# Moving the stationary operands of the token-major products 32 bytes below the weights' place within 512 bytes

## The chip, the cores and the metric

The program runs on one core of one Trainium2 chip. The metric is the device time of one execution in microseconds, as the median of several runs. One more execution was recorded by the hardware profiler, and all rows below come from that one.

## The reference

Two transformer blocks are chained on 256 tokens of width 1024. All of it is float32.

```python
# block 1, two layers
for layer in range(2):
    xn = rms_norm(h, attn_norm_g[layer])
    u_ssm, u_g, v_g, q, k, v = split(xn @ w_in[layer])          # 256,256,256,512,512,512 columns
    mixed = concat([s5_mixer(u_ssm), spatial_gating(u_g, v_g), diff_attention(q, k, v)])
    h = h + mixed @ w_out[layer]
    xn = rms_norm(h, ffn_norm_g[layer])
    a = causal_conv3(xn @ w_up[layer])                          # 2 x 2816 columns
    gate, val = split(a)
    h = h + (gelu(gate) * val) @ w_down[layer]
# block 2, one layer
n = rms_norm(x, g_pre)
a_qkv, bq, bk, bv, mq, ga, gb, gm, mg = split(n @ w_in_2)       # 12 chunks of 512 for a, mg and so on
branches = [windowed(a_qkv) * silu(ga), grouped(bq, bk, bv) * silu(gb), memory(mq, mem) * silu(gm)]
merged = sum(sigmoid(mg_i + b_i) * (branch_i @ w_br_i))
out = x + rms_norm(merged @ w_out, g_post)
```

## The kernel before

**The stream of weights.** All the large products share one stream of 294 pairs of weight tiles. A pair is 128 partitions by 1024 float32 columns (512 KB). The SP queue loads it into `raw` (one of 7 slots). ScalarE rounds it to a high part `whi` (6 slots, L1177), VectorE makes the rest, `wlo = raw - whi` (7 slots, in the memory of `raw`, L1873). The activations are split in the same way into a high and a low part: the normed input into `xthb` and `xtlb`, the gated units into `hth` and `htl`, the branch outputs into `oth` and `otl`, the normed memory into `memh` and `meml`. TensorE then makes three products in `fp32r` for each tile: high by high, high by low, low by high.

**Two forms of product.** `project` and `pair_products` issue them in one of two forms.

- Feature-major (`fm=True`, L646 to L648): the *weights* are the stationary operand (128 columns, 512 bytes of a partition) and the *activations* are the moving one, 256 columns (1024 bytes). This form serves `ssm_u`, the 22 `up` units but one, `km`, `mq`, `gb`, `gm` and `ga`.
- Token-major (L655 to L657 in `pair_products`, and L603, L593, L586 in `tile_pairs`, which makes one tile of tokens at a time): the *activations* are stationary (128 columns, 512 bytes) and the *weights* move, 512 columns (2048 bytes). This form serves q, k, gmlp, v, out, down, `up0_0`, vm, bq, the nine chunks of a, mg, the branch products and wo. `bkv` has this form with 256 moving columns.

Each matmul has a load of its stationary operand of its own (LDWEIGHTS, shown as engine PEld), and the load for the next matmul runs while the present one streams.

**Two places for the normed input.** `xthb` and `xtlb` each hold the normed input at one of two offsets: `xth`, `xtl` at offset 0 and `fth`, `ftl` at offset 8 elements, which is 32 bytes. The first is what attention, mixer, output and second-block products read; the second is written by the norm ahead of the up products and read by them alone.

```python
(xth, xtl), (fth, ftl) = ([b[:, o:o + KD * TOK].rearrange("p (k n) -> p k n", k=KD) for b in (xthb, xtlb)]
                          for o in (0, 8))
```

**Places within 512 bytes.** SBUF tensors are laid out one behind the other, so a start is the sum of the sizes ahead of it. Three unused tensors (`lines`, `lines1`, `lines2`) fill up to a multiple of 512 bytes. With the sizes in the code, the starts modulo 512 are these (the low parts lie as the high ones):

| tensor | bytes within 512, before | after |
|---|---|---|
| `whi`, `wlo` (all slots), `xres`, `xn` | 0 | 0 |
| `xth`, `xtl` | 0 | 480 |
| `fth`, `ftl` | 32 | 32 |
| `memh`, `meml` | 0 | 0 |
| `hth`, `htl`, `acc`, `gtd` | 0 | 480 |
| `aqT`, `va`, `oth`, `otl`, `merged`, `gpost` | 0 | 480 |
| `kmT`, `vm`, `colv` | 64 | 480 |
| `rowv`, `cst` (identity, rotation tables) | 384 | 288 |

**Order of work.** The order on every engine is written out by hand; small products and transposes of attention and of the mixer are set between the pairs of the stream. Nothing of that order depends on where a tensor lies.

Of the kernel before, what the change touches and what calls it, by code (L numbers as in the profile page):

```python
# [20 lines left out]
P = 128  # L21
TOK, TT = 256, 2
D, KD = 1024, 8
# [14 lines left out]
F32, F32R = mybir.dt.float32, mybir.dt.float32r  # L38
# [101 lines left out]
def build(nc, weights, x, mem, cols, rows, lams, bmerge, consts, amask, bexp, cexp, wst, wglu, out):  # L140
    with ExitStack() as ctx:
        def sbt(stack, name, shape, dt=F32):
            return stack.enter_context(nc.sbuf_tensor(name, shape, dt))
# [3 lines left out]
        def sem(name):  # L147
            if name not in sems:
# [10 lines left out]
        xres = sbt(ctx, "xres", [P, TT, D])  # L159
        xn = sbt(ctx, "xn", [P, TT, D])  # L160
        xthb = sbt(ctx, "xthb", [P, KD * TOK + 128], F32R)
        xtlb = sbt(ctx, "xtlb", [P, KD * TOK + 16], F32R)
        (xth, xtl), (fth, ftl) = ([b[:, o:o + KD * TOK].rearrange("p (k n) -> p k n", k=KD) for b in (xthb, xtlb)]
                                  for o in (0, 8))
        kmT = sbt(ctx, "kmT", [P, MH, TOK])
        vm = sbt(ctx, "vm", [P, TT, 512])

# [17 lines left out]
        hb = sbt(ctx, "hb", [P, 4])  # L185
        nlam = sbt(ctx, "nlam", [P, LAYERS])
        lamv = sbt(ctx, "lamv", [P, 8])
        sbt(ctx, "lines", [P, 120])

        def col(name, i=0, n=None):  # L190
            a, b = COL[name]
# [66 lines left out]
        mix.close()  # L258
        ffs = ExitStack()
        one.enter_context(ffs)  # L260
        sbt(ffs, "lines1", [P, 96])
        hth = sbt(ffs, "hth", [P, FT, TOK], F32R)
        htl = sbt(ffs, "htl", [P, FT, TOK], F32R)
        acc = sbt(ffs, "acc", [P, 2, 4, TOK])
# [5 lines left out]
        two = ExitStack()  # L270
# [15 lines left out]
        mqT = sbt(bm, "mqT", [P, MH, TOK])  # L286
        bm.close()
        gt = sbt(two, "gt", [P, TT, 3 * D])
        sbt(two, "lines2", [P, 96])
        att = ExitStack()  # L290
        two.enter_context(att)
        aqT = sbt(att, "aqT", [P, 2, NG, 4, TOK])
# [2348 lines left out]
```

## Time and profile before

| | us |
|---|---|
| median of 3 runs | 965.48 (964.66 to 966.56) |
| span of the profiled execution | 964.3 |
| mean granted TensorE clock | 0.999 of full |

The profiled execution is known by its span; the median of the runs lies 1.2 us above it. In the rows, PE is TensorE's matmul queue and PEld its loads of the stationary operand. The time shown for one matmul includes its way through the pipeline, so several overlap: what one costs in a stream is the distance between two starts, and this is how the rows are used here.

### The profile page before, as it was taken

Reading aid. Unit: us, or ns where it says so; the run is one execution under the profiler, and the core shown is the slowest. Engines: PE = TensorE matmul, PEld = TensorE weight load, DVE = VectorE, ACT = ScalarE, POOL = GpSimd, SP = SyncE. Lnnn points to the kernel's source line nnn. Section 1 sums busy time; section 2 is a strip of 40 time slices with the busy share of each in tenths; the row PEclk is TensorE's granted clock in tenths of the full one; section 3 lists DMA queues with packets and bytes.
Section 4 is the critical chain, followed back from the end, with each engine's and each line's share of the span. In section 5 each row is a group of like instructions: output and inputs, shape, how many; then the busy total and the mean of one; then the engine's idle time right before and its main releaser. Section 6 shows DMA issues by size and latency. Waiting matters only on the chain.

```text
span 964.3 us, 15784 instructions
## 1 busy us (share of the span) xinstructions
PE 953.3 (99%) x6119; PEld 837.1 (87%) x6123; DVE 687.4 (71%) x1081; ACT 567.6 (59%) x960; POOL 232.1 (24%) x189
## 2 busy tenths in 40 slices
PE   8999999999999999999999999999999999999997
PEld 6887899999888888899999988999778889888886
DVE  7987878786765877857777754748576755666885
ACT  7967666676855657756666544535454445555733
POOL 5560203536500110302445500021131300000030
PEclk9999999999999999999999999999999999999999
DMA  8642466656664634466566565665545445754462
GB/s 299 227 131 68 142 219 186 189 178 184 194 197 152 180 127 153 133 188 192 180 194 178 195 196 154 216 202 173 166 139 153 153 144 170 199 162 155 154 180 82
DMA packets 48618, 165.96 MB, mean 172 GB/s; under 512 B 6560, under 2 KB 7072, under 8 KB 48544
## 3 DMA queue, kind: packets, MB, share of 16 engines
q1 hardware_dynamic: 48544, 164.95, 54.9%
q8 instruction: 49, 0.80, 0.3%
q14 instruction: 25, 0.20, 0.1%
HBM read 162.83 MB, written 1.05 MB: 170 GB/s over the span
## 4 chain that ended last, share of the span: by engine, by line
PE 88%; ACT 4%; POOL 3%; DVE 3%; issue 1%; DMA 1%; SPq 0%; DVEq 0%; POOLq 0%; ACTq 0%
PE PJ L655 14%; PE PJ L657 13%; PE PJ L656 13%; PE PJ L648 10%; PE PJ L647 10%; PE PJ L646 10%; PE PJ L593 2%; PE PJ L603 2%; PE PJ L586 2%; PE T L1118 1%; ACT sm L1378 1%; PE T L1109 1%; ACT whi L1177 1%; DMA raw<-weights_in 1%; DVE wlo L1873 1%
## 5 line engine op out<-in xcount | busy, mean ns | idle before, releaser
L1873 DVE TENSOR_TENSOR wlo<-raw,whi 128x1024 fp32r<-128x1024 f32 x294 | 368.7, 1284 | 87.2 <-ACT whi L1177 84.8
L1177 ACT ACTIVATE whi<-raw 128x1024 fp32r<-128x1024 f32 x294 | 301.6, 1059 | 64.9 <-DMA raw<-weights_in 62.5
L646 PE MATMUL PJ<-xthb,whi 128*128 128x256 f32 x832 | 233.7, 281 | 0.0
L648 PE MATMUL PJ<-xthb,wlo 128*128 128x256 f32 x832 | 233.4, 281 | 0.0
L647 PE MATMUL PJ<-xtlb,whi 128*128 128x256 f32 x832 | 232.4, 279 | 0.0
L655 PE MATMUL PJ<-whi,xthb 128*128 128x512 f32 (+1 forms) x424 | 170.8, 403 | 0.3 <-DVE wlo L1873 0.2
L657 PE MATMUL PJ<-whi,xtlb 128*128 128x512 f32 (+1 forms) x424 | 164.0, 387 | 0.0
L656 PE MATMUL PJ<-wlo,xthb 128*128 128x512 f32 (+1 forms) x424 | 164.0, 387 | 0.0
L647 PEld LDWEIGHTS PJ<-xtlb,whi 128*128 128x128 f32 x832 | 157.0, 189 | 0.3
L646 PEld LDWEIGHTS PJ<-xthb,whi 128*128 128x128 f32 x832 | 157.0, 189 | 0.3
L648 PEld LDWEIGHTS PJ<-xthb,wlo 128*128 128x128 f32 x832 | 156.9, 189 | 0.0
L1798 POOL TENSOR_TENSOR gtd<-acc 128x512 f32<-128x512 f32 x22 | 93.6, 4255 | 166.4 <-ACT acc L1502 158.7
L2256 DVE SCALAR_TENSOR_TENSOR acc<-PJ,colv,acc 128x255 f32<-128x255 f32 (+1 forms) x168 | 69.2, 475 | 48.6 <-ACT acc L1497 47.9
L655 PEld LDWEIGHTS PJ<-whi,xthb 128*128 128x128 f32 x424 | 79.7, 188 | 20.5 <-issue 4.3
L657 PEld LDWEIGHTS PJ<-whi,xtlb 128*128 128x128 f32 x424 | 79.7, 188 | 16.8
L656 PEld LDWEIGHTS PJ<-wlo,xthb 128*128 128x128 f32 x424 | 79.9, 188 | 14.0
L1497 ACT ACTIVATE acc<-PJ,colv 128x256 f32<-128x256 f32 x84 | 40.6, 564 | 77.6 <-PE PJ L648 77.6
L655 PE MATMUL PJ<-whi,hth 128*128 128x512 f32 x144 | 56.0, 389 | 0.0
L657 PE MATMUL PJ<-whi,htl 128*128 128x512 f32 x144 | 56.0, 389 | 0.0
L656 PE MATMUL PJ<-wlo,hth 128*128 128x512 f32 x144 | 56.0, 389 | 0.0
L1852 POOL TENSOR_TENSOR merged<-merged,gt 128x512 f32<-128x512 f32 x6 | 9.6, 1625 | 160.7 <-DVE gt L2482 160.7
L657 PEld LDWEIGHTS PJ<-whi,htl 128*128 128x128 f32 x144 | 27.0, 188 | 5.7
(419 smaller groups left out, 1353.2 us busy)
## 6 DMA issues: line engine op xcount, KB each, us to landing
raw<-weights_in SPq DMA_DIRECT2D x294, 512.0 KB, 3.6
rt<-bmerge_in SPq DMA_DIRECT2D x6, 256.0 KB, 4.1
memx<-mem_in SPq DMA_DIRECT2D x2, 512.0 KB, 4.0
y_out<-xn SPq DMA_DIRECT2D x4, 256.0 KB, 2.3
rowv<-rows_in SPq DMA_DIRECT2D x1, 576.0 KB, 10.5
xres<-x_in SPq DMA_DIRECT2D x2, 256.0 KB, 3.0
xres<-x_in SPq DMA_DIRECT2D x1, 512.0 KB, 7.7
ptmp<-bexp_in SPq DMA_DIRECT2D x2, 256.0 KB, 6.0
```

The source lines that it names most:

```text
L586: m = pe.matmul(o, lw, wh, start=False, stop=stop and kk == 1, skip_group_check=True)
L646: pe.matmul(o, a, xh[:, k, :], start=(first and f % 2 == 0), stop=False, skip_group_check=True)
L647: pe.matmul(o, a, xl[:, k, :], start=False, stop=False, skip_group_check=True)
L648: m = pe.matmul(o, b, xh[:, k, :], start=False, stop=last, skip_group_check=True)
L655: pe.matmul(o, h, wh, start=first, stop=False, skip_group_check=True)
L656: pe.matmul(o, h, wl, start=False, stop=False, skip_group_check=True)
L657: m = pe.matmul(o, lw, wh, start=False, stop=last, skip_group_check=True)
L1177: act.activation(whi[:, p % HIGHS, :], raw[:, p % LOADS, :], ACT.Copy).then_inc(hi_ready, 1)
L1497: act.activation(acc[:, j % 2, i, :], banks[i // 2][:, (i % 2) * TOK:(i % 2 + 1) * TOK], ACT.Identity, scale=colv[:, k + 2:k + 3], bias=co ...
L1798: pool.tensor_tensor(gtd[:, j % 2, :, :], acc[:, j % 2, 0:2, :], acc[:, j % 2, 2:4, :], ALU.mult).then_inc(sem("gated"), 1)
L1873: dve.tensor_tensor(wlo[:, p % LOADS, :], raw[:, p % LOADS, :], whi[:, p % HIGHS, :].bitcast(F32), ALU.subtract).then_inc(lo_ready, 1)
L2256: dve.scalar_tensor_tensor(out=acc[:, j % 2, i, sh:TOK], in0=banks[i // 2][:, (i % 2) * TOK:(i % 2 + 1) * TOK - sh], scalar=colv[:, k + ta ...
```

## The change

It moves `xth`/`xtl` from offset 0 to offset 120 elements (480 bytes, 32 below the next multiple of 512), lengthens `xtlb` so that it has room for that, and shortens the three fillers. `lines1` and `lines2` are now 32 bytes shorter, which puts `hth`/`htl` and `oth`/`otl` at 480 within 512. `lines` is shortened so that everything behind it starts where it did; the small tensors between `xtlb` and `lines` lie 416 bytes further on. No instruction is added, removed or put in another order.

```diff
-        xtlb = sbt(ctx, "xtlb", [P, KD * TOK + 16], F32R)
+        xtlb = sbt(ctx, "xtlb", [P, KD * TOK + 120], F32R)
         (xth, xtl), (fth, ftl) = ([b[:, o:o + KD * TOK].rearrange("p (k n) -> p k n", k=KD) for b in (xthb, xtlb)]
-                                  for o in (0, 8))
+                                  for o in (120, 8))
...
-        sbt(ctx, "lines", [P, 120])
+        sbt(ctx, "lines", [P, 16])
...
-        sbt(ffs, "lines1", [P, 96])
+        sbt(ffs, "lines1", [P, 88])
...
-        sbt(two, "lines2", [P, 96])
+        sbt(two, "lines2", [P, 88])
```

## Rows read from the trace of the kernel before

**Rows 1.** The page: span, busy time of TensorE, shares of the last chain.

```profile
span 964.3 us, 15784 instructions
PE 953.3 (99%) x6119; PEld 837.1 (87%) x6123; DVE 687.4 (71%) x1081; ACT 567.6 (59%) x960; POOL 232.1 (24%) x189
PE 88%; ACT 4%; POOL 3%; DVE 3%; issue 1%; DMA 1%; SPq 0%; DVEq 0%; POOLq 0%; ACTq 0%
```

**Rows 2.** Waits of TensorE: total us, times, longest.

```profile
PE PJ L890 <- POOL mT L1752: 1.9, 1, 1.9
PE PJ L603 <- ACT xthb L1200: 0.7, 1, 0.7
PE PJ L603 <- ACT whi L1177: 0.6, 1, 0.6
...
PE PJ L655 <- DVE wlo L1873: 0.2, 1, 0.2
```

**Rows 3.** Groups of TensorE by form: busy us, mean ns, idle before.

```profile
L646 PE MATMUL PJ<-xthb,whi 128*128 128x256 f32 x832 | 233.7, 281 | 0.0
...
L655 PE MATMUL PJ<-whi,xthb 128*128 128x512 f32 x408 | 166.3, 407 | 0.2
...
L655 PE MATMUL PJ<-whi,hth 128*128 128x512 f32 x144 | 56.0, 389 | 0.0
...
L603 PE MATMUL PJ<-whi,xthb 128*128 128x512 f32 x88 | 28.1, 401 | 1.4 <-ACT xthb L1200 0.7 <-ACT whi L1177 0.6
...
L655 PE MATMUL PJ<-whi,oth 128*128 128x512 f32 x48 | 19.0, 395 | 0.0
...
L603 PE MATMUL PJ<-whi,hth 128*128 128x512 f32 x32 | 9.9, 392 | 0.0
...
L655 PE MATMUL PJ<-whi,xthb 128*128 128x256 f32 x16 | 4.6, 287 | 0.2 <-DVE wlo L1873 0.2
```

**Rows 4.** Timeline of TensorE, feature-major `mq`: start, us; 12 starts apart.

```profile
618.74 0.28 PE L646 MATMUL PJ<-xthb,whi 128*128 128x256 f32 x1
...
620.18 0.28 PE L646 MATMUL PJ<-xthb,whi 128*128 128x256 f32 x1
```

**Rows 5.** The same, up units of the first layer; 15 starts apart.

```profile
159.75 0.28 PE L646 MATMUL PJ<-xthb,whi 128*128 128x256 f32 x1
...
161.50 0.28 PE L646 MATMUL PJ<-xthb,whi 128*128 128x256 f32 x1
```

**Rows 6.** The same, up units of the second layer; 51 starts apart.

```profile
430.09 0.28 PE L647 MATMUL PJ<-xtlb,whi 128*128 128x256 f32 x1
...
436.09 0.28 PE L647 MATMUL PJ<-xtlb,whi 128*128 128x256 f32 x1
```

**Rows 7.** Timeline of TensorE, token-major `down`; 33 starts apart.

```profile
264.22 0.39 PE L655 MATMUL PJ<-whi,hth 128*128 128x512 f32 x1
...
271.70 0.39 PE L655 MATMUL PJ<-whi,hth 128*128 128x512 f32 x1
```

**Rows 8.** The same, first pairs of an a chunk, from the burst's start.

```profile
698.21 0.50 PE L655 MATMUL PJ<-whi,xthb 128*128 128x512 f32 x1
698.54 0.39 PE L656 MATMUL PJ<-wlo,xthb 128*128 128x512 f32 x1
...
699.70 0.39 PE L655 MATMUL PJ<-whi,xthb 128*128 128x512 f32 x1
...
703.55 0.39 PE L657 MATMUL PJ<-whi,xtlb 128*128 128x512 f32 x1
```

**Rows 9.** The same, token-major `up0_0`, reading `fth`; two matmuls a row.

```profile
123.53 0.63 PE L593 MATMUL PJ<-wlo,xthb 128*128 128x512 f32 x2
...
126.80 0.63 PE L586 MATMUL PJ<-whi,xtlb 128*128 128x512 f32 x2
```

**Rows 10.** Windows, TensorE: stretch, length, busy (count), clock, DMA share, GB/s.

```profile
9.00:106.00 97.00, 94.05 (x595) 1.00 0.51 170
106.00:310.00 204.00, 204.00 (x1402) 1.00 0.60 189
```

**Rows 11.** The last chain: transposes of `vm` and of `xn`, eight each.

```profile
209.96 0.87 PE S L721 x8
...
303.82 0.87 PE S L702 x8
```

**Rows 12.** Windows, VectorE at L1891 alone, writing `xtl` and then `ftl`.

```profile
10.00:60.00 50.00, 4.40 (x16) 1.00 0.65 227
106.00:130.00 24.00, 4.40 (x16) 1.00 0.56 179
```

## The prediction

> **What bounds the kernel now.** The page comes first: TensorE has a matmul in flight for 953.3 of 964.3 us, and the chain of work that ended last is TensorE's for 88% of the span [rows 1]. A busy share of 99% could still hide waits, so the list of waits is next. TensorE waited for another engine only a few times, the longest 1.9 us once at the start, the rest 0.7 us and less [rows 2]. The kernel is therefore as long as the sum of the distances between starts of matmuls, and any change of one such distance goes through to the end, except where a short wait would appear in its place.
>
> So I measured the distance in a steady stream for each pair of operands, and put beside it where the two operands lie within 512 bytes. "Above" means moving operand minus stationary operand.
>
> | stream | moving above stationary | distance, ns | from |
> |---|---|---|---|
> | feature-major `mq` | 0 | 1.44 us / 12 = 120.0 | [rows 4] |
> | feature-major up, layer 0 | +32 | 1.75 / 15 = 116.7 | [rows 5] |
> | feature-major up, layer 1 | +32 | 6.00 / 51 = 117.6 | [rows 6] |
> | token-major `down` | 0 | 7.48 / 33 = 226.7 | [rows 7] |
> | token-major a chunk, settled | 0 | 3.85 / 17 = 226.5 | [rows 8] |
> | token-major `up0_0` | -32 | 3.27 / 14 = 233.6 | [rows 9] |
>
> [...] The same instruction with the same shape takes 3.3 or 2.4 ns less when its moving operand lies 32 bytes above the stationary one. It takes 6.9 ns more when it lies 32 below. [...] The granted clock is full in all these stretches [rows 10], so it is not the clock. The load of the next stationary operand runs during the present matmul, and the place of one against the other is all that differs.
>
> **The change, part by part.** It changes only spacings, so each stream is looked up in that table.
>
> *Token-major products, stationary operand moved down by 32.* With the stationary operand at 480, the moving weights at 0 lie +32 above it, the same relation that the up units have. The counts come from the groups, three lines to each: normed input 3 x (408 + 88) = 1488, less the 48 of `up0_0`, is 1440; gated units 3 x (144 + 32) = 528; branch outputs 3 x 48 = 144; together 2112 [rows 3]. No row shows this form at +32. From above, its gain is bounded by the up units of layer 0, 120.0 - 116.7 = 3.3 ns; from below, by the one other token-major row off 0, 6.9 ns more [rows 9]. I take 3.0 ns less, between the two up streams (3.3 and 2.4) and nearer the first. [...] 2112 x 3.0 = -6.3 us. Bounds: -7.0 and +14.6 us.
>
> *`bkv`*, token-major with 256 columns: 3 x 16 = 48 [rows 3], at -3 ns each -0.1 us.
>
> *Feature-major products on `xth`.* Here the roles are exchanged: the weights are stationary at 0 and `xth` moves at 480, so the spacing becomes -32, the one that costs in `up0_0`. These are `ssm_u` twice, `mq`, `gb`, `gm` and `ga`: 3 x 832 = 2496 feature-major matmuls [rows 3], less 21 up units x 96 = 2016 on `fth`, leaves 480 (`km` reads `memh` and is apart). No row shows this form at -32. The bounds are 3.3 ns less (any offset helps this form) and 6.9 ns more [rows 4, 5, 9]. I take 6.9 more, since that row has the same sign of spacing and both forms agree at 0: 480 x 6.9 = +3.3 us. Bounds -1.6 and +3.3 us.
>
> *Up units, `up0_0`, `km`, `vm`.* Spacing unchanged: `fth` stays at 32 and `memh` at 0. Nothing.
>
> *Bursts.* After small products a token-major stream needs some matmuls to settle: 698.54 to 699.70 is 5 distances of 232 ns, 27 ns over the settled rate in all [rows 8]. With some 40 bursts that is about 1 us, and the new spacing may give some of it back or as much again. I take nothing and put 1 us on either side of the range.
>
> *Everything else that moves.* The identity in `cst` goes from 384 to 288, `kmT` and `vm` from 64 to 480, `aqT`, `va`, `merged`, `acc` from 0 to 480. The transposes of `vm` (at 64) and of `xn` (at 0) against the same identity both take 0.87 us for eight [rows 11], so their rate does not follow the spacing. VectorE's L1891 takes 4.40 us for 16 whether it writes at 0 or at 32 bytes [rows 12]. Both cost nothing here. If the plain small products did follow the spacing, by 3 ns either way over some 500 of them, it would be 1.5 us.
>
> *What a faster TensorE runs into.* From 9 to 106 us TensorE is busy 94.05 of 97 us and its waits lie there [rows 2, 10]: rounding, vector and GpSimd work of the mixer comes just in time. Of the 240 token-major matmuls there, 0.7 us of gain, I count 0.3 as lost to such waits. From 106 to 310 us the share is 204.00 of 204.00: the weight stream keeps ahead, and the 12 token-major matmuls of a pair shrink by only 12 x 3.0 = 36 ns of 12 x 226.7 = 2720. A later wait is not likely.
>
> Sum: -6.3 - 0.1 + 3.3 + 0.3 = -2.8 us. On the span of 964.3 that is 961.5; the median stood 1.2 above the span, so 962.7 us.
>
> [...]
>
> **The rivals.**
>
> *B: feature-major does not pay.* The token-major gain comes, and the 480 feature-major matmuls at -32 stay at 120 or gain. For it: they are another shape than the row at -32. Against it: the sign. 965.5 - 6.4 + 0.3 + (0 to -1.6) = 959.4 to 957.8.
>
> *C: token-major has no gain.* With 512 moving columns the load covers only part of the stream, so the rate at 0 may already be the best this form has, while feature-major pays at -32: +3.3 us, 968.8. For it: no token-major row is below 226.5. [...]
>
> *D (the other side): token-major pays for any offset.* One mechanism: the token-major stream is in step with its loads only at spacing 0, and 32 bytes either way break it. Its place is each of the 2112 distances, its price up to 6.9 ns, which makes +14.6 us, and with the feature-major term 965.5 + 17.9 = 983.4 at most. It decides from where the token-major price passes zero: with +3.3 us from feature-major, a token-major gain under 1.5 ns already makes the kernel no faster. For it: the only off-zero row of this form is slower. Against it: feature-major shows that the sign of the spacing counts.
>
> *E: the change does not do what it says.* The operands are moved but the distances stay, as they would if placement had no part in the differences of the table and something else, such as what lies in PSUM or the order of high and low, made them. For it: `up0_0` also issues in another order than L655 to L657, two matmuls of each kind in a row. Against it: `down`'s last pairs have that order and the groups show no such cost (L603 on `hth`, mean 392 ns against 389) [rows 3]. 965.5.
>
> **How the numbers follow.** The forecast (token-major gains 2.2 to 3.3, feature-major pays 5 to 7) has 0.50; B 0.21; C 0.11; D 0.13; E 0.05. Within the forecast the time goes from 965.5 - 7.1 + 2.4 = 960.8 to 965.5 - 4.7 + 3.3 + 0.3 = 964.4. The range reaches from B's better end to C with the effect of bursts left out, 957.8 to 969.0; what is outside is D, and a little beyond B. About 0.2% (1.9 us) is what a measurement of this kernel can tell from no change: faster is below 963.6. Of the forecast's 0.50, 0.40 lies there, and with B that makes 0.61 faster; within 0.2% are 0.10 of the forecast, E and 0.03 of D, 0.18; slower are C and most of D, 0.21.
>
> **What would show each step.** In the timeline of the changed kernel, `down` and the settled a chunks should start every 223 to 224.5 ns; above 226.7 is D, at 226.7 C. `mq` and `ga` should start every 127 ns; 120 or less is B. The up units stay at 116.7 and 117.6, `up0_0` at 233.6, transposes of eight at 0.87 us. TensorE's waits before 106 us may grow by some 0.3 us. The prediction fails most if the token-major distance is wrong, since 2112 matmuls stand on a rate that no row of that form shows: each ns there is 2.1 us.

## The result and the profile after

The changed kernel takes 974.29 us (median of 4, 973.88 to 975.18) against 965.52 us of the kernel before on the same chip: ratio 1.0089, 95% interval 1.0076 to 1.0101. It is 8.8 us slower, where 2.8 us less was forecast, and lies above the stated range of 957.8 to 969.0. The profiled execution has a span of 972.6 us, 8.3 above that of before. The page of the changed kernel, span and busy times:

```profile
span 972.6 us, 15784 instructions
PE 962.4 (99%) x6119; PEld 835.8 (86%) x6123; DVE 687.3 (71%) x1081; ACT 567.9 (58%) x960; POOL 232.9 (24%) x189
```

VectorE, ScalarE and GpSimd work as long as before [rows 1]; TensorE has 9.1 us more. Its waits, in the list of waits of the changed kernel, are not longer than in [rows 2]:

```profile
PE PJ L890 <- POOL mT L1752: 1.9, 1, 1.9
PE PJ L603 <- ACT whi L1177: 0.6, 1, 0.6
PE T L702 <- DVE xn L1882: 0.5, 1, 0.5
PE PJ L655 <- ACT whi L1177: 0.4, 1, 0.4
```

So the distances between starts changed. The timeline of TensorE in the changed kernel shows where. First `down`, 30 starts apart, to be held against [rows 7]:

```profile
266.02 0.39 PE L655 MATMUL PJ<-whi,hth 128*128 128x512 f32 x1
...
273.02 0.39 PE L655 MATMUL PJ<-whi,hth 128*128 128x512 f32 x1
```

7.00 / 30 = 233.3 ns where it was 226.7. Then the first pairs of an a chunk, as in [rows 8], from its second matmul:

```profile
703.19 0.39 PE L656 MATMUL PJ<-wlo,xthb 128*128 128x512 f32 x1
...
708.32 0.39 PE L657 MATMUL PJ<-whi,xtlb 128*128 128x512 f32 x1
```

That is 5.13 us for 22 distances, 233.2 ns. Before, 698.54 to 703.55 was 5.01 us for as many, 227.7 with the settling included. And `mq`, feature-major, 21 starts apart, against [rows 4]:

```profile
623.41 0.28 PE L646 MATMUL PJ<-xthb,whi 128*128 128x256 f32 x1
...
625.90 0.28 PE L646 MATMUL PJ<-xthb,whi 128*128 128x256 f32 x1
```

2.49 / 21 = 118.6 ns where it was 120.0. `bkv`, token-major with 256 columns, 12 starts apart:

```profile
656.62 0.28 PE L655 MATMUL PJ<-whi,xthb 128*128 128x256 f32 x1
...
658.02 0.28 PE L655 MATMUL PJ<-whi,xthb 128*128 128x256 f32 x1
```

1.40 / 12 = 116.7 ns: the one token-major product with 256 moving columns gained. The table takes all distances between two neighbouring matmuls of a family from both traces, save those that hold a pause (300 ns and more with 512 columns, 150 ns and more with 256):

| family | before, ns | after, ns | matmuls | difference, us |
|---|---|---|---|---|
| token-major, normed input, 512 columns | 228.5 | 233.1 | 1440 | +6.7 |
| token-major, gated units | 226.8 | 233.3 | 528 | +3.4 |
| token-major, branch outputs | 227.3 | 233.3 | 144 | +0.9 |
| feature-major, normed input at `xth` | 119.9 | 118.3 | 480 | -0.7 |
| `bkv` | 119.6 | 116.8 | 48 | -0.1 |
| up units (spacing unchanged) | 117.3 | 117.3 | 2016 | 0 |

The sum is +10.2 us, the span grew by 8.3. Most of the rest is in the first 132 us. The timeline of the changed kernel has the second half of the first pair of `up0_1` here:

```profile
132.13 0.36 PE L646 MATMUL PJ<-xthb,whi 128*128 128x256 f32 x1
```

In the kernel before it is 132.26. Some 290 slower matmuls, 1.3 us, lie ahead of it and cost nothing, as TensorE filled idle time with them. The window of the changed kernel that answers to [rows 10] has 1.09 us more of busy time in the same 97 us for the same work:

```profile
9.00:106.00 97.00, 95.14 (x596) 1.00 0.50 169
```

### The profile page after: what moved, and what is told of

Same layout as the page of the kernel before. It is cut to its first block, busy times and chain, and to the rows that moved or that the text cites. A ratio compares the mean times of both kernels' runs of the same rounds, so it can differ in the third digit from the quotient of the medians.

```text
span 972.6 us, 15784 instructions
## 1 busy us (share of the span) xinstructions
PE 962.4 (99%) x6119; PEld 835.8 (86%) x6123; DVE 687.3 (71%) x1081; ACT 567.9 (58%) x960; POOL 232.9 (24%) x189
## 4 chain that ended last, share of the span: by engine, by line
PE 94%; DVE 3%; ACT 2%; DMA 1%; issue 0%; SPq 0%; DVEq 0%; POOLq 0%; POOL 0%; ACTq 0%
PE PJ L655 15%; PE PJ L656 14%; PE PJ L657 14%; PE PJ L648 10%; PE PJ L646 10%; PE PJ L647 10%; PE PJ L586 3%; PE PJ L593 3%; PE PJ L603 3%; PE T L1118 1%; DVE wlo L1873 1%; PE T L756 1%; PE T L1109 1%; DMA raw<-weights_in 1%; PE S L1074 1%; PE T L1047 1%
## 5 line engine op out<-in xcount | busy, mean ns | idle before, releaser
L646 PE MATMUL PJ<-xthb,whi 128*128 128x256 f32 x832 | 233.4, 280 | 0.0
L648 PE MATMUL PJ<-xthb,wlo 128*128 128x256 f32 x832 | 233.1, 280 | 0.0
```

The source lines that it names most:

```text
L646: pe.matmul(o, a, xh[:, k, :], start=(first and f % 2 == 0), stop=False, skip_group_check=True)
L648: m = pe.matmul(o, b, xh[:, k, :], start=False, stop=last, skip_group_check=True)
```

## The experiments

**Which part of the change costs.** Two kernels take one half of the change each, a third moves the normed input the other way.

`only_units` undoes the move of the normed input:

```diff
-                                  for o in (120, 8))
+                                  for o in (0, 8))
```

> The changed kernel with the normed input back at 0; only gated units and branch outputs stay 32 bytes below. Theory of shape: 528 + 144 token-major matmuls pay 6.6 ns each, +4.4 us over the kernel before, about 970.0 us. Rival, the small tensors that moved (identity, tables) carry the loss: about 974 us, since they stay moved here.

Measured: 970.01 us against 965.36, ratio 1.0046 (1.0031 to 1.0061), +4.65 us, as expected by shape. The family of gated units is at 233.3 ns, that of the normed input back at 228.5.

`only_input` undoes the other half:

```diff
-        sbt(ffs, "lines1", [P, 88])
+        sbt(ffs, "lines1", [P, 96])
...
-        sbt(two, "lines2", [P, 88])
+        sbt(two, "lines2", [P, 96])
```

> The changed kernel with gated units and branch outputs back at 0; only the normed input stays 32 bytes below. Theory of shape: 1440 token-major matmuls pay 4.6 to 6.6 ns (the stream before was not always settled), less what is hidden before 106 us, 432 feature-major and 48 bkv matmuls gain 1.5 and 3 ns: +4.5 to +7.5 us over the kernel before, 970 to 973 us. Together with the run of the units alone the two losses add up to the whole, 8.8 us. Rival, small tensors: about 974 us here as well, and the two losses add up to more than the whole.

Measured: 970.36 us, ratio 1.0045 (1.0028 to 1.0062), +5.0 us, within what shape expected. The two losses add up to 9.65 us, the whole was 8.8; each ratio is uncertain by some 1.5 us, so they add up within the noise. The rival had the small tensors, which are moved in both kernels, carry the loss, and asked for 974 us in both. They carry nothing that can be seen: in the changed kernel the transposes still take 0.87 us for eight.

`input_above` is the kernel before with one number changed:

```diff
-                                  for o in (0, 8))
+                                  for o in (8, 8))
```

> The kernel before with the normed input at 32 bytes above instead of 0, in the place of the up units' input; all else as before, no small tensor moves. Theory of shape, the sign does not matter: within 1.5 us of the run with the normed input 32 below (970 to 973 us). Rival, the sign counts as the prediction had it, only with the other sign for the token-major form: the token-major distance differs from 233.4 ns and the feature-major one is 116.7 instead of 118.3 ns.

Measured: 969.76 us, ratio 1.0042 (1.0027 to 1.0057), 0.6 us from `only_input`, where within 1.5 was expected. The token-major family is at 233.1 ns, as with the normed input 32 below (233.2). The sign does not matter for this form at 32 bytes. The feature-major family is at 116.7 against 118.3, so there the sign does count a little.

**What the place does, apart from the kernel.** `map_spacing` is a kernel with nothing but streams of matmuls, each with a load of its own. It, the two grids and `cells_long` below leave out the whole computation and ran once each. Stationary and moving operand alternate between neighbouring tiles:

```python
for i, (a, b, n) in enumerate(((0, 0, 512),) + STREAMS):
    for j in range(BEATS):
        s = j % 2 * P
        m = j // 2 % 2 * 512
        k = pe.matmul(acc[i % 2][:, 0:n], still[a][:, s:s + P], moving[b][:, m:m + n],
                      start=(j == 0), stop=(j == BEATS - 1), skip_group_check=True)
```

> This kernel leaves out the whole computation: it makes only streams of 48 fp32r matmuls each, one stream per spacing between moving and stationary operand, with 128, 256, 384 and 512 moving columns, and stores a copy of part of the input. Theory of shape: the spacing alone counts, whatever the role or the absolute place; with 512 columns a spacing of 0 gives 226.7 ns and 32 bytes either way 233.4 ns; with 256 columns 0 gives 120 ns and 32 either way 117 to 118.5 ns; both operands moved by 32 together give the values of spacing 0 (226.7 and 120). Rival, absolute place: the stream slows when the activation's own place leaves 0; then both operands at 32 give 233.4 ns with 512 columns, and only the stationary operand's place moves the rate. Larger spacings are shown by no row: if the conflict repeats every 64 or 128 bytes, spacings of 64, 128 and 256 give the value of 0; if it repeats only every 512, they differ.

The theory's figures are in the grids below, as (stationary, moving): with 512 columns 226.7 ns at (0, 0), 233.2 at (0, 32) and 233.3 at (32, 0); with 256 columns 120.0 at (0, 0), 116.6 at (0, 32) and 118.1 at (32, 0). With both operands at 32 they have 226.7 and 120.0, the values of (0, 0), and not the 233.4 of the rival. That the spacing alone counts is too much: both at 16 had 230.0 and 118.4.

This kernel's labels were wrong, and so were two things that I read from it. Tensors are laid out in steps of 32 bytes, and my fillers of 16 bytes were rounded up, so that most stationary tensors lay above their label: the one called 16 was at 32, 32 at 64, 48 at 96, 64 at 128, 96 at 160, 128 at 192, 192 at 256, 448 at 0, 480 at 32 and 496 at 64. With true places its settled distances for 512 columns are 226.7 at 0 and 256, 233.4 at 32 and 64, 232.3 at 128, 228.8 at 192. The grids below bear the true places out: the stream labelled 128 had 228.8, and the grid has 232.7 at 128 and 228.8 at 192; the one labelled 496 had 113.3 with 256 columns, and the grid has 120.3 at 496 and 113.3 at 64. "Both at 32" was in truth moving at 32 and stationary at 64, and gave the 233.4 of a difference of 32, so it says nothing for the absolute place. With 384 columns it had 173.3 at 0 and at 32 and 176.7 at 64; with 128 columns 111.7 at each of these three places. The stationary operand at 64 with 256 columns showed both 117.8 and 113.3 ns, in two streams.

Two grids put this right. One large stationary and one large moving tile, both starting at the same place within 512, are read at offsets in steps of 16 bytes, all 32 x 32 combinations.

```diff
-        s = j % 2 * P
-        m = j // 2 % 2 * 512
+        s = a // 4 + j % 2 * P
+        m = b // 4 + j // 2 % 2 * 512
```

> Leaves out the whole computation: only streams of 18 fp32r matmuls with 256 moving columns, one for each place of the stationary operand (32 steps of 16 bytes within 512) and each place of the moving one (32 steps). The first map had a stationary operand at 496 and a moving one at 0 at 113.3 ns, and both at 32 at 118.3 instead of 120. Theory of spacing (the difference modulo 512 decides): each diagonal of the grid has one value, 113.3 on the diagonal with the moving operand 16 bytes above, 120 on the main one. Rival, two places: the places count each by itself; then (0, 16) is not 113.3 and the main diagonal is 120 in some cells only.

> The same with 512 moving columns and 16 matmuls to a stream. Theory of spacing: one value to a diagonal, 226.7 ns at differences 0, 64 and 320 of the moving above the stationary operand, 233.4 at 32 either way. Rival, two places: the first map had both operands at 32 at 233.4 ns, so the main diagonal is 226.7 in some cells only; which cells those are shows whether the stationary operand's own place must be a certain one. Either way the grid says whether any cell is below 226.7 ns.

The first rows or columns of both grids, as the mean of nine (256 columns) or six (512 columns) distances from the seventh on:

| bytes | feature-major case: 256 columns, stationary 0, moving at | token-major case: 512 columns, moving 0, stationary at |
|---|---|---|
| 0 | 120.0 | 226.7 |
| 16 | 118.6 | 233.3 |
| 32 | 116.6 | 233.3 |
| 48 | 118.4 | 233.3 |
| 64 | 117.8 | 233.3 |
| 80 | 119.7 | 231.7 |
| 96 | 119.7 | 234.3 |
| 112 | 114.0 | 233.3 |
| 128 | 119.2 | 232.7 |
| 144 | 118.3 | 226.7 |
| 160 | 117.7 | 234.3 |
| 176 | 119.2 | 229.2 |
| 192 | 117.8 | 228.8 |
| 208 | 119.7 | 231.5 |
| 224 | 118.2 | 233.2 |
| 240 | 117.1 | 226.7 |

From 256 to 496 the columns repeat within 0.2 ns, save for the first stream of all (226.7 at 0 and 228.7 at 256). Over the whole of both grids, moving the stationary operand by 256 changes practically no cell by more than 0.3 ns, and moving the moving one by 256 leaves 94% of the cells within 0.3 ns. So the pattern's period is 256 bytes, not 512; some of the others differ by up to 4.4 and 6.7 ns, as cells with two rhythms would (see `cells_long`). No cell of the grids is below 113.3 or 226.7.

Moving both operands by 32 keeps 95% of the cells within 0.3 ns, moving both by 16 does not: a difference of 112 gave 114.0 with the stationary operand at 0 and 120.1 with it at 16. Neither theory holds entirely: with the stationary operand at a multiple of 32 the difference decides in most cells (a difference of 32 has 116.6 to 116.7 ns with 256 columns and 233.2 to 233.3 with 512), and with it at an odd multiple of 16 another pattern holds (the same difference has 118.1 to 118.3 and 232.2 to 232.3). Two expected values came from the wrong labels and were missed: with 256 columns the moving operand 16 above has 118.6 ns, not 113.3, and with 512 columns and the stationary operand at a multiple of 32, differences of 64 and 320 have some 229, not 226.7.

**A first try of a cell in the kernel** ran with the grids, before they were known. `up_16` moves only the up units' input:

```diff
-                                  for o in (0, 8))
+                                  for o in (0, 4))
```

> The whole kernel before with one number changed: the up units' input 16 bytes above the weights instead of 32. Theory of spacing: 2016 feature-major matmuls start every 113.3 ns instead of 116.7 to 117.7, -3.4 to -4.4 ns each, -7 to -9 us, 956.5 to 958.5 us if ScalarE and VectorE keep up with pairs of 24 x 113.3 = 2.72 us. Rival, two places: the moving operand at 16 with the stationary one at 0 is another cell than 496 with 0, the distance stays between 116 and 119 ns and the time within 2 us of the kernel before, 963.5 to 967.5.

Measured: 965.17 us, ratio 0.9993 (0.9984 to 1.0003), no difference. The mean of the up family is 117.1 ns (117.3 before), but it is not one rate. The units `up0_2` to `up0_7` run at 113.3 ns, as hoped; 15 starts apart:

```profile
198.02 0.28 PE L646 MATMUL PJ<-xthb,whi 128*128 128x256 f32 x1
...
199.72 0.28 PE L646 MATMUL PJ<-xthb,whi 128*128 128x256 f32 x1
```

Then sixteen transposes (L721) stand in the order. Behind them the same stream, at the same places, runs at 118.7 ns to the end of the layer, and so does all of layer 1; again 15 starts apart:

```profile
212.18 0.28 PE L646 MATMUL PJ<-xthb,whi 128*128 128x256 f32 x1
...
213.96 0.28 PE L646 MATMUL PJ<-xthb,whi 128*128 128x256 f32 x1
```

1.70 / 15 = 113.3 and 1.78 / 15 = 118.7. The gain of the six units, 576 x 3.4 = 2.0 us, is mostly taken back by the slower ones. The two `PJ` accumulators take turns from unit to unit on both sides of the transposes, so they do not choose the rate. The expected 113.3 came from the wrong label of 496, so that six units had it was luck; the grid's 118.6 for this cell, a short stream, did not show that it has a faster rhythm too.

**Cells picked from the grid, in the kernel.** `up_112` is the kernel before with the up units' input at 112 bytes:

```diff
-        xtlb = sbt(ctx, "xtlb", [P, KD * TOK + 16], F32R)
+        xtlb = sbt(ctx, "xtlb", [P, KD * TOK + 32], F32R)
...
-                                  for o in (0, 8))
+                                  for o in (0, 28))
...
-        sbt(ctx, "lines", [P, 120])
+        sbt(ctx, "lines", [P, 104])
```

> The kernel before with one place changed: the up units' input 112 bytes above the weights instead of 32. The grid has 114.0 ns for the moving operand at 112 with 256 columns, against 116.6 at 32 and 120.0 at 0. Theory that the grid's cell decides, also in the whole kernel: 2016 matmuls at 113.3 to 114.0 instead of 117.3 ns, -6.5 to -8 us, 957.5 to 959 us. Rival, in the whole kernel something else sets the distance (other engines' reads, the burst from which the stream starts): the distance stays near 117 ns and the time within 1.5 us of the kernel before.

The small tensors between `xtlb` and `lines` lie 64 bytes further on. Measured: 958.52 us against 965.57, ratio 0.9928 (0.9914 to 0.9941), as the grid had it. The timeline of TensorE in the up units of layer 0, 15 starts apart as in [rows 5]:

```profile
149.95 0.28 PE L646 MATMUL PJ<-xthb,whi 128*128 128x256 f32 x1
...
151.65 0.28 PE L646 MATMUL PJ<-xthb,whi 128*128 128x256 f32 x1
```

1.70 / 15 = 113.3 ns. Its family mean is 113.5 against 117.3, and 2016 x 3.8 = 7.7 us is about what the span lost (964.3 to 956.7). Here the units on both sides of the sixteen transposes run at 113.3.

`up_112_input_240` puts the normed input of all other products at 240 bytes too (`for o in (60, 28)`, with `xtlb` 64 elements longer than its data and `lines` at 72).

> The same, and the normed input of all other products at 240 bytes instead of 0. The grid has 226.7 ns for 512 columns with the stationary operand at 240 (as at 0), and 117.1 for 256 columns with the moving operand at 240 (120.0 at 0). Theory of the grid: the token-major products stay at 226.7 ns, 480 feature-major ones gain 2.9 ns, -1.4 us, so 956 to 957.5 us, 1 to 1.5 below the run with 112 alone. Rival: 240 holds 226.7 ns only in the grid's short streams; then 1440 matmuls pay up to 6.6 ns and the time is up to 9 us above the run with 112 alone.

Measured: 957.74 us, ratio 0.9919 (0.9905 to 0.9932), the lowest median of this study. Its lead of 0.8 us over `up_112` (1 to 1.5 were expected) is inside the intervals; the trace supports it. An a chunk in its timeline, 18 starts apart:

```profile
691.16 0.39 PE L655 MATMUL PJ<-whi,xthb 128*128 128x512 f32 x1
...
695.24 0.39 PE L655 MATMUL PJ<-whi,xthb 128*128 128x512 f32 x1
```

4.08 / 18 = 226.7 ns, as the grid had it. `mq` has 18 starts from 613.86 to 615.97 us, 117.2 ns against 120.0.

`up_96` is `up_112` with 24 in place of 28 elements (`xtlb` + 24, `lines` at 112), to see whether the grid also forecasts a loss.

> The kernel before with the up units' input at 96 bytes instead of 32. The grid has 119.7 ns there, 16 bytes from the best cell. Theory of the grid: 2016 matmuls lose 2.4 ns each, +4.9 us, 970 to 971 us. Rival (any place off 0 is as good with 256 columns as any other): 964.5 to 966.5 us.

Measured: 971.36 us, ratio 1.0060 (1.0046 to 1.0074), 0.4 above what was expected. The up family is at 120.0 ns. Sixteen bytes make 12.8 us between these two kernels.

**Does a cell have one rate?** `cells_long` has 16 cells with 96 matmuls each, in one order and then in reverse.

> Leaves out the whole computation: 16 cells of the grid as streams of 96 matmuls, once in one order and once in the reverse order, so that each follows another stream. Theory that a cell has one rate: both times the same, 120.0 at (0,0), 116.6 to 117.8 at (0,32), 119.7 at (0,96), 113.3 to 114.0 at (0,112), 226.7 for 512 columns at (0,0), (240,0), (144,0), 233.3 at (32,0), (480,0), (112,0). Rival, a cell has more than one steady rhythm and the stream before decides: then some cell, most likely (64,0) or (0,192), which is the same difference and had 113.3 and 117.8 in the grid, shows two values.

Its windows on TensorE; the count of a window includes the two or so matmuls that are in flight at its left edge. The first five are streams with 256 columns, at (stationary, moving) = (0, 0), (0, 32), (0, 96), (0, 112), and (0, 32) again in the reverse order. The last four have 512 columns: (32, 0), (240, 0), (144, 0), and (144, 0) in the reverse order:

```profile
31.00:40.00 9.00, 9.00 (x77) 1.00 0.00 0
42.00:51.00 9.00, 9.00 (x79) 1.00 0.01 2
54.00:63.00 9.00, 9.00 (x77) 1.00 0.01 2
66.00:75.00 9.00, 9.00 (x82) 1.00 0.01 2
519.00:528.00 9.00, 9.00 (x80) 1.00 0.01 2
154.00:173.00 19.00, 19.00 (x83) 1.00 0.00 1
199.00:218.00 19.00, 19.00 (x85) 1.00 0.00 0
221.00:240.00 19.00, 19.00 (x85) 1.00 0.00 1
332.00:351.00 19.00, 19.00 (x83) 1.00 0.00 1
```

In equal time (0, 112) starts five matmuls more than (0, 0) or (0, 96), and (0, 32) starts one more in its second pass. The mean distances of these passes are 120.0, 117.8, 120.0, 113.5 and 116.7; then 233.4, 226.7, 226.7 and 233.3. So the rival is right for some cells: (0, 32) with 256 columns and (144, 0) with 512 have two steady rhythms. The other 14 cells kept one value in both passes, (0, 0), (0, 112) and (240, 0) among them. (0, 192), one of the two for which I expected it, had 113.3 in both passes here and 117.8 in the grid; (64, 0), the other, had 113.3 in both passes and in the grid, and 117.8 in one stream of `map_spacing`.

The two passes differ in the stream that runs before, and also in the accumulator, as a cell's second pass always writes the other one of `acc`. The accumulator alone does not choose the rhythm: (144, 0) was in `acc1` at 226.7 in the grid and in `acc1` at 233.3 in the second pass. With the switch behind the transposes in `up_16`, this makes what ran before the likely reason; what in it decides is open.

## Why the prediction was wrong, point by point

**What bounds the kernel: right.** TensorE is the path, and each distance goes through to the end but for the first 132 us. There the forecast had 0.3 us hidden; it was some 1.3 us. The granted clock was given with [rows 10], which end at 310 us; in the windows 430 to 440, 618 to 622 and 698 to 704 us of the same trace, where the other streams of the table lie, it is 1.00 as well.

**The token-major term: wrong, and this is the step that failed.** It said -6.3 us, from the gains of the up streams, and held against rival D that "feature-major shows that the sign of the spacing counts". It came out at +11.0 us (6.7 + 3.4 + 0.9). The sign does not matter for 512 columns at 32 bytes: 233.3 ns below, 233.1 above. What I took for the effect of the sign was that of the number of moving columns. The one table I had confounded them: every row with a gain had 256 columns and lay at +32, the only loss had 512 columns and lay at -32. That "both forms agree at 0", as the feature-major term has it, no row ahead of the prediction shows. The runs have it in this sense: at spacing 0, 256, 384 and 512 columns take 120.0, 173.3 and 226.7 ns (grids, `map_spacing`), so each further 128 columns cost 53.3 ns, and what is left beside the columns is some 13.3 ns in all three. But it says nothing of places off 0: at 32 it is the number of columns that decides (with the stationary operand there, 118.1 ns with 256, 173.3 with 384, 233.3 with 512).

**The feature-major term: wrong sign.** It said +3.3 us; it came out at -0.7. With 256 columns 32 bytes either way help (118.3 below, 116.7 to 117.8 above).

**`bkv`: right**, -0.1 us, and in the changed kernel it is the telling case: token-major by role, 256 columns, and it gained. Before, it lay at spacing 0 like the others and could not decide; but it was in my groups, and I priced it with the token-major products without asking whether the role or the column count sets the price.

**Rival D** named this outcome, "token-major pays for any offset", with 0.13, and had nearly the right token-major price (6.9 against 6.6 ns); its total of 983.4 was too high by the feature-major term, the hidden part, and the unsettled bursts: the normed input's family was at 228.5 ns before, not 226.7, so it had less to lose. That the stream is "in step with its loads only at spacing 0" is too broad: 144 and 240 had 226.7 ns as well, and no run shows that it is in step with its loads at all. It was right for the one place that the change used. **Rival B**'s feature-major half was right as well.

**Everything else that moves: right.** The transposes kept 0.87 us for eight and VectorE's L1891 its 4.40 us for 16, and the small tensors cost nothing that can be seen.

**Rival E: wrong.** In the grids the streams alone went from 113.3 to 122.7 ns with 256 columns and from 226.7 to 235.2 with 512 by place only, so placement has its part. The runs do not show that one read waits for the other.

Why the number of columns decides is not settled. A load takes 0.19 us in the trace before, in both forms. The timeline of its loads, first in `mq`, then in `down`:

```profile
621.02 0.19 PEld L648 LDWEIGHTS PJ<-xthb,wlo 128*128 128x128 f32 x1
621.14 0.19 PEld L646 LDWEIGHTS PJ<-xthb,whi 128*128 128x128 f32 x1
...
268.07 0.19 PEld L655 LDWEIGHTS PJ<-whi,hth 128*128 128x128 f32 x1
268.30 0.19 PEld L656 LDWEIGHTS PJ<-wlo,hth 128*128 128x128 f32 x1
```

With 256 columns 0.19 us is more than the distance of 0.12, so two loads overlap; with 512 it is less than 0.23, as rival C had it ("the load covers only part of the stream"). No run tests whether this is the reason. In the grids the rate depends on the places of both operands; what ties the two together, no run shows.

## What to carry to other kernels

Where a stream of fp32r matmuls with a load for each is the bound, the place of the stationary against the moving operand was worth some 5% of its time with 256 columns (120.0 to 113.3 ns) and 3% with 512 (233.3 to 226.7), and it can be had for a few bytes of offset. Don't carry a good place from one shape to another (the moving operand 32 bytes above took 120.0 to 116.6 ns with 256 columns and 226.7 to 233.2 with 512): measure a small grid of places for each number of moving columns, which took two short kernels here, and then confirm the cell in the kernel, stretch by stretch: a cell can have two rates, as in `up_16`, and a family's mean hides it. Before leaning on a table of a few rows, ask which two properties change together in it, and look for a case that takes them apart (here `bkv` at 32, or one short stream with 512 columns at +32).

## What was not expected of the hardware

- The distance between matmuls repeats with a period of 256 bytes in the operands' places (with 256 columns and the stationary operand at 0, 114.0 ns with the moving one at 112 and at 368), and 16 bytes, the finest step that was tried, can change it: at 256 columns 119.7 ns at 96 bytes and 114.0 at 112.
- The best cells were 113.3 ns for 256 columns (120.0 with both operands at 0) and 226.7 ns for 512, which is also that of both at 0.
- With 128 columns the places tried, the stationary operand at 0, 32 and 64, made no difference (111.7 ns); with 384 columns 32 bytes cost nothing (173.3) and 64 bytes cost 3.4 ns (176.7).
- Some cells have two steady rhythms for the same instructions (113.3 or 118.7 in `up_16`, 226.7 or 233.3 in `cells_long`), and the switch in `up_16` stands behind sixteen transposes. The up units of both layers lie at the same spacing and run at 116.7 and 117.6 ns [rows 5, 6]; these are about the two values of the cell (0, 32), 116.7 and 117.8.
